# Matrix-LSTM key blocks overlapped with rows fetched by DMA, and the first attention's norm two heads later

## The reference

```python
# first block: the two attention outputs are normed and joined
mixed = jnp.concatenate([_rmsnorm(o_a, norm_fox_out[l]), _rmsnorm(o_b, norm_sb_out[l])], axis=-1)
# o_a: forgetting attention ("fox"); o_b: stick-breaking attention ("sb"), 8 heads

# second block: matrix LSTM, 4 heads of 96, once forward and once backward
dmat = jnp.where(tri, b[..., :, None] - b[..., None, :] + ib[..., None, :], -jnp.inf)
m_t = jnp.maximum(inter, dmat.max(axis=-1))
s = jnp.einsum("bhtd,bhsd->bhts", qb, kb) * jnp.exp(dmat - m_t[..., None])
...
h = num / jnp.maximum(jnp.abs(den), jnp.exp(-m_t))[..., None]
...
h = h_f + h_b
h = h * lax.rsqrt(jnp.mean(h * h, axis=-1, keepdims=True) + EPS)
h = h.reshape(B, N, M_WIDTH) * g_m * jax.nn.sigmoid(mo)
```

## Time and profile before

| | us |
|---|---|
| median of 3 runs | 1767.93 (1761.85 to 1769.10) |
| the profiled execution | 1768.98 |
| its span in the profile | 1767.2 |
| PE busy | 1677.7 (95%) |
| DVE busy | 1110.0 (63%) |
| ACT busy | 804.0 (45%) |
| POOL busy | 84.1 (5%) |
| mean granted PE clock | 0.969 |

### The profile page before, as it was taken

The page is one execution under the profiler, slowest core; times in us unless marked ns, Lnnn a source line. Parts: engine busy times, 40 slices in busy tenths (PEclk is TensorE's granted clock), DMA queues, the critical chain, the costliest instruction groups (busy, mean ns, idle before and its releaser), DMA issues.

```text
span 1767.2 us, 27194 instructions
## 1 busy us (share of the span) xinstructions
PE 1677.7 (95%) x9914; PEld 1398.0 (79%) x9914; DVE 1110.0 (63%) x1808; ACT 804.0 (45%) x1318; POOL 84.1 (5%) x140
## 2 busy tenths in 40 slices
PE   7999888999999999999899999999999998999997
PEld 7987477899999977766337788888887875589997
DVE  5544677768888888634665755555558835475564
ACT  5534444454444454344563542144225355566462
POOL 0000000000001000000200000000000001000000
PEclk9999899999999999999789999999999998799999
DMA  7634244357777732410003355455542420046562
GB/s 279 207 114 132 82 141 158 131 166 251 248 239 246 243 105 72 131 60 0 1 1 131 126 199 163 142 179 190 158 147 81 130 85 0 1 144 202 172 197 83
DMA packets 68921, 244.64 MB, mean 138 GB/s; under 512 B 7392, under 2 KB 10608, under 8 KB 68720
## 3 DMA queue, kind: packets, MB, share of 16 engines
q1 hardware_dynamic: 54000, 189.43, 32.2%
q0 software_dynamic: 14848, 54.21, 9.9%
HBM read 242.55 MB, written 1.06 MB: 138 GB/s over the span
## 4 chain that ended last, share of the span: by engine, by line
PE 80%; DVE 11%; ACT 5%; issue 3%; DMA 1%; DVEq 0%; SPq 0%; ACTq 0%
PE pair L948 79%; DVE uv L1596 1%; DVE wl L1556 1%; ACT wh L472 1%; DVE sq L1574 1%; DVE sq L1632 1%; PE pair L1116 1%; DVE small L1623 1%; DVE uh_f L1669 1%; ACT sq L500 1%; DVE ul L1585 1%; ACT sq L844 1%; ACT rstd L510 0%; ACT rstd L512 0%; ACT sq L542 0%
## 5 line engine op out<-in xcount | busy, mean ns | idle before, releaser
L948 PE MATMUL pair<-uh,wh 128*128 128x256 f32 (+3 forms) x1840 | 577.5, 314 | 16.1 <-DVE ul L1585 7.1
L1556 DVE TENSOR_TENSOR wl<-ring,wh 128x1024 fp32r<-128x1024 f32 x350 | 426.8, 1224 | 243.2 <-ACT wh L472 236.4
L948 PE MATMUL pair<-ul,wh 128*128 128x256 f32 (+3 forms) x1840 | 572.5, 311 | 0.0
L948 PE MATMUL pair<-uh,wl 128*128 128x256 f32 (+3 forms) x1840 | 572.2, 311 | 0.0
L472 ACT ACTIVATE wh<-ring 128x1024 fp32r<-128x1024 f32 x350 | 367.6, 1052 | 265.1 <-PE pair L948 261.4
L948 PEld LDWEIGHTS pair<-uh,wh 128*128 128x128 f32 (+1 forms) x1840 | 342.8, 186 | 50.8 <-issue 18.1
L948 PEld LDWEIGHTS pair<-uh,wl 128*128 128x128 f32 (+1 forms) x1840 | 342.9, 186 | 25.1
L948 PEld LDWEIGHTS pair<-ul,wh 128*128 128x128 f32 (+1 forms) x1840 | 342.7, 186 | 24.0
L948 PE MATMUL pair<-hh,wh 128*128 128x512 f32 (+1 forms) x512 | 172.6, 337 | 0.8
L948 PE MATMUL pair<-hl,wh 128*128 128x512 f32 (+1 forms) x512 | 172.0, 336 | 0.0
L948 PE MATMUL pair<-hh,wl 128*128 128x512 f32 (+1 forms) x512 | 172.0, 336 | 0.0
(11 more groups left out here) (254 smaller groups left out, 2197.8 us busy)
## 6 DMA issues: line engine op xcount, KB each, us to landing
ring<-in_w_stream SPq DMA_DIRECT2D x350, 512.0 KB, 3.9
uh_f<-in_mods POOLq DMA_DIRECT2D x48, 512.0 KB, 6.1
mod_w<-in_mods POOLq DMA_DIRECT2D x48, 512.0 KB, 3.8
table<-in_table SPq DMA_DIRECT2D x1, 1849.5 KB, 12.4
res<-in_x SPq DMA_DIRECT2D x4, 256.0 KB, 3.7
res<-in_mem SPq DMA_DIRECT2D x1, 1024.0 KB, 14.7
res<-in_ctx POOLq DMA_DIRECT2D x1, 1024.0 KB, 6.3
uv<-c_rows POOLq DMA_DIRECT2D x2, 512.0 KB, 6.6
```

The lines of the kernel that those rows point to most:

```text
L948: ins = pe.matmul(*operands, **flags)
L1556: tt(wl[:, s, :], ring[:, s, :], wh[:, s, :].bitcast(F32), ALU.subtract).then_inc(S("w_lo"), 1)
```

## The change

**Rows by transfer.** For each layer GpSimd writes the rows of both directions to a new DRAM tensor `ml_dram`. It reads each head's row of both directions back, repeated on 128 partitions, twice (`row_load`, 512 KB each): one copy for blocks 0 and 2, one for blocks 1 and 3, where masks are added in place. There are buffers for two heads; the loads of heads 2 and 3 wait until heads 0 and 1 have left theirs (`ml_e`), and they stand behind the 16 casts in GpSimd's queue. The row maximum comes likewise (`max_load`). `spread`, `head_m` and ACT's copies (L853) go.

**1/den by transfer.** For heads 0 to 2, GpSimd writes 1/den to `den_dram` and, once that has landed (`den_out`), reads it back over 96 partitions into `quot` (`quot_in`). Head 3 is still spread by PE (`last_spread`).

**Order.** PE makes the scores of block t + 1 ahead of the values of block t; DVE adds masks one block ahead. Both directions go in one instruction where they can. Head h's square, norm, root and value now run two heads later. The rounding of the other mixers' results moves into head 0's steps. In the output projection head 2's norm stands before k = 4 and `last_spread` before k = 6.

**Forgetting attention's norm.** PE's part moves from h == 2 to h == 4, ACT's root from 2 to 5, DVE's gain from 4 to 6; squares and their sum stay.

Of the loops over the four heads the diff shows the new lines only; the old loops stand in the listing above.

```diff
+        ML_STEPS = [(h, kb) for h in range(MH) for kb in range(4)]
...
-        rb, arg = [ml[:, d, :] for d in range(2)], [ml[:, 4 + d, :] for d in range(2)]
-        den, quot = [ml[MD:MD + 1, 2 + d, :] for d in range(2)], [ml[0:MD, 6 + d, :] for d in range(2)]
+        rb_even = [lw[:, 0:1024].rearrange("p (d t) -> p d t", d=2), ml[:, 0:2, :]]
+        rb = [rb_even, [ml[:, 2:4, :], ml[:, 4:6, :]]] * 2
+        mrow = mrow_at[MD:MD + 1]
+        den, quot = ml[MD:MD + 1, 6:8, :], ml[0:MD, 6:8, :]
...
+            def row_load(l, h, k):
+                if h >= 2:
+                    pool.wait_ge(S("ml_e"), 8 * (l * MH + h - 1))
+                pool.dma_start(rb[h][k], ml_dram[l, :, h, 0, :].rearrange("(o d) t -> o d t", o=1)
+                               .to_broadcast([P, 2, 512])).then_inc(S(f"rb_in{h}_{k}"), 16)
+            def max_load(l, h):
+                if h >= 2:
+                    pool.wait_ge(S("ml_min"), l * MH + h - 1)
+                k = 2 * (h % 2)
+                pool.dma_start(mrow[:, k:k + 2, :], ml_dram[l, :, h, 1, :].rearrange("(o d) t -> o d t", o=1)
+                               ).then_inc(S(f"max_in{h % 2}"), 16)
+            def den_spread(l, h):
+                out = den_dram[l, h, :, cols].rearrange("(o d) t -> o d t", o=1)
+                pool.wait_ge(S("ml_rden"), l * MH + h + 1)
+                pool.dma_start(out, den[:, :, cols]).then_inc(S("den_out"), 16)
+                pool.wait_ge(S("den_out"), 16 * (l * (MH - 1) + h + 1))
+                if h:
+                    pool.wait_ge(S("u_v"), value_count(f"y_{l}", MH + 2 + h - 1))
+                pool.dma_start(quot[:, :, cols], out.to_broadcast([MD, 2, cols.stop - cols.start])
+                               ).then_inc(S("quot_in"), 16)
             for l in range(NL):
                 cols = lin_cols(l)
+                for d in range(2):
+                    pool.wait_ge(S("ml_rows"), 2 * l + d + 1)
+                    pool.dma_start(ml_dram[l, d], rows[d][:, 3:5, :]).then_inc(S("rows_out"), 16)
+                pool.wait_ge(S("rows_out"), 32 * (l + 1))
+                pool.wait_ge(S("job_full"), JOBS.full(JOBS.number(f"va_{l}", 3)))
+                row_load(l, 0, 0)
+                for h in range(2):
+                    max_load(l, h)
+                pool.wait_ge(S("sm_s"), UNIT0["mlat1"] if l == 0 else len(UNITS))
+                pool.wait_ge(S("conv_done"), 8 * l + 8)
+                for h, k in ((0, 1), (1, 0), (1, 1)):
+                    row_load(l, h, k)
                 for j in range(2):
                     pool.wait_ge(S("u_l"), U_AT[f"y_{l}"] + MH + j + 1)
                     for q in range(4):
                         for dst, src in ((uh, yfh), (ul, yfl)):
                             pool.tensor_copy(dst[MD:P, 4 * j + q, cols],
                                              src[32 * q:32 * q + 32, j, cols]).then_inc(S("y_moved"), 1)
+                for h in range(MH - 1):
+                    if h + 2 < MH:
+                        for k in range(2):
+                            row_load(l, h + 2, k)
+                    den_spread(l, h)
+                    if h + 2 < MH:
+                        max_load(l, h + 2)
...
                 if h == 2:
                     for t in range(2):
                         square("fox", t, heads[:, 2 * t:2 * t + 2, :], P, 512)
+                if h == 5:
                     root("fox", P, T, 512)
...
+                def head_root(h):
+                    root(f"head_{l}_{h}", MD, n, MD)
...
+                act.wait_ge(S("sm_out"), units.stop)
+                for h, kb in ML_STEPS:
+                    exps(h, kb)
+                    if h == 0 and kb < 3:
+                        round_y(2 * kb)
+                        round_y(2 * kb + 1)
+                    if kb == 0 and h >= 2:
+                        head_square(h - 2)
+                    if kb == 1 and h >= 2:
+                        head_root(h - 2)
+                    if kb == 1 and h:
                         head_ln(h - 1)
+                    if kb == 2 and h:
+                        head_exp(h - 1)
+                    if kb == 2 and h >= 2:
                         head_round(h - 2)
                 head_ln(MH - 1)
+                head_square(MH - 2)
+                head_exp(MH - 1)
+                head_root(MH - 2)
                 head_round(MH - 2)
                 head_square(MH - 1)
+                head_root(MH - 1)
                 head_round(MH - 1)
...
-                if h == 2:
+                if h == 4:
                     pe.wait_ge(S("sm_out"), NF)
                     wait_emptied(pe, "xkv", 7)
...
+                def head_norm(h):
+                    norm(f"head_{l}_{h}", MD, n)
+                def last_spread():
+                    pe.wait_ge(S("ml_rden"), (l + 1) * MH)
+                    pe.wait_ge(S("norm_rstd"), NORM[f"head_{l}_{MH - 2}"] + 1)
                     for d in range(2):
+                        last = mm(bank[6 + d][0:MD, cols], ones[MD:MD + 1, 0:MD], den[:, d, cols], start=True, stop=True)
+                    last.then_inc(S("ml_bc"), 1)
+                for j in range(4):
+                    claim(f"mlstm_{l}", j)
+                keys(0, 0)
+                for t, (h, kb) in enumerate(ML_STEPS):
+                    if t + 1 < len(ML_STEPS):
+                        keys(*ML_STEPS[t + 1])
+                    if kb == 0 and h >= 2:
+                        pe.wait_ge(S("ml_sum"), l * MH + h - 1)
+                    values(h, kb)
+                    if kb == 0 and h >= 2:
+                        head_norm(h - 2)
                 s = p0 + N_IN2
...
-                for k in range(4):
+                for k in range(KT - 1):
+                    if k == 4:
+                        head_norm(MH - 2)
+                    if k == 6:
+                        last_spread()
                     for m in range(2):
                         output(early[m], m, k)
-                head_spread(MH - 1)
-                for k in range(4, KT - 1):
-                    for m in range(2):
-                        output(early[m], m, k)
-                norm(f"head_{l}_{MH - 1}", MD, n)
+                head_norm(MH - 1)
                 for m in range(2):
...
-                if h == 4:
+                if h == 6:
...
+                    a = rb[h][kb % 2]
+                    dve.wait_ge(S(f"rb_in{h}_{kb % 2}"), 16 * (l + 1))
                     for d in range(2):
-                        if kb == 0:
-                            dve.wait_ge(S("ml_b_in"), 2 * (l * MH + h) + d + 1)
-                        if kb:
-                            dve.wait_ge(S("ml_e"), 2 * (4 * (l * MH + h) + kb - 1) + d + 1)
-                        tc = CTX if kb < 2 else LAT
-                        tt(arg[d][:, tc], rb[d][:, tc], masks[d][:, kb % 2, :], ALU.add).then_inc(S("ml_arg"), 1)
+                        if kb >= 2:
+                            dve.wait_ge(S("ml_e"), 2 * (t - 2) + d + 1)
+                        tt(a[:, d, c], a[:, d, c], masks[d][:, kb % 2, :], ALU.add).then_inc(S("ml_arg"), 1)
...
+                    if h < MH - 1:
+                        dve.wait_ge(S("quot_in"), 16 * (l * (MH - 1) + h + 1))
+                    else:
+                        dve.wait_ge(S("ml_bc"), l + 1)
+                        ch.link(dve.tensor_copy(quot[:, :, cols],
+                                                pair[3][0:MD, :].rearrange("p (d t) -> p d t", d=2)[:, :, cols]))
+                    ch.link(tt(quot[:, :, cols], ml_pair(l, h)[0:MD, :, cols], quot[:, :, cols], ALU.mult))
...
+                args(0, 0)
+                for t, (h, kb) in enumerate(ML_STEPS):
+                    if t + 1 < len(ML_STEPS):
+                        args(*ML_STEPS[t + 1])
+                    if kb == 2 and h:
                         head_min(h - 1)
+                    weigh(h, kb)
+                    if h == 0 and kb < 3:
+                        rest_y(2 * kb)
+                        rest_y(2 * kb + 1)
+                    if kb == 1 and h >= 2:
+                        head_value(h - 2)
+                    if kb == 2 and h >= 2:
+                        head_rest(h - 2)
+                    if kb == 3 and h:
                         head_sum(h - 1)
                 head_min(MH - 1)
+                head_value(MH - 2)
```

171 lines of the change are left out of this document (45 added, 126 removed).

## The result

The changed kernel takes 1775.38 us (median of 8 runs, 1771.73 to 1781.70), the kernel before 1768.13 beside it (8 runs, 1761.85 to 1770.44). The ratio is 1.0052 with a 95% interval of 1.0033 to 1.0071: slower by half a per cent, where the prediction had 1767 and a slight gain. The range (1754 to 1781) holds the time; the direction is wrong.

What follows compares the result with a forecast made beforehand. PE, busy 95%, bounds the whole; in the three stretches touched, waits, the lower clock and a serial chain do. Terms -8.3 + 6.1 + 0.2 = -2.0 from the profiled 1768.98 give 1767.0 us; range 1754 to 1781.

Steps and rivals of the forecast that it cites:

- The stick-breaking stage, -8.3 us: Stick-breaking stage: the norm's move removes PE's 3.97 us wait; head 5's copy comes at 215.5 against 223.8.
- this takes the clock to stay at 1.00 once the wait is gone: Stick-breaking stage: the condition for -8.3 us; if the clock still drops, about -1.
- the first attention's norm brings little: Rival, stick-breaking stage: the clock still drops or the wait moves elsewhere, -1 instead of -8.3, 1774 us; chance 0.12.
- Layer 0, +6.1 us: Layer 0's matrix LSTM: late row load, two trips and longer tail outweigh the overlap; last row group 944.1 against 937.96.
- The loop: Layer 0's matrix LSTM: each head's serial loop takes 19.6 us with the trip, 21.5 at the low clock.
- The tail: End of layer 0's matrix LSTM: from head 3's first weighing at 900.7 to the last row group at 944.1.
- The round trip, 6.3 us: 1/den through DRAM in the matrix LSTM: 2.8 write plus 3.5 read; bounds 5.6 and 12.0; 5.9 in layer 1.
- Layer 1, +0.2 us: Layer 1's matrix LSTM: the same at half width; last row group at 1548.4 against 1548.20.
- The dearer trip: Rival, GpSimd's queue: six trips in the matrix LSTMs, each from 2.5 us more, +15, 1782 us; chance 0.18.
- The clock rival: Rival, matrix LSTMs: the clock stays up, the low-clock terms of 11.4 us go, 1755.6 us; chance 0.25.
- the overlap doesn't work: Rival, matrix LSTMs: exponentials still form the chain, only costs come, about 12 us more, 1779 us; chance 0.05.
- The rule of the Trainium skill: GpSimd's transfers: 2.0 us fixed plus bytes over 436 GB/s, 3.2 for 512 KB; a trip some 4.9, result near 1759.

Runs made afterwards that it cites:

- a_loads: The changed kernel with head 2's two row loads ahead of GpSimd's 16 casts, the first 1/den still behind them; 1764.68 us, 0.9984 of before.
- a_casts: The changed kernel with head 2's row loads first and GpSimd's casts behind the 1/den of heads 0 and 1, eight each; 1758.13 us, 0.9948 of before.
- e_pe2: a_casts with every head's 1/den spread by TensorE, no transfer of it, the spread ahead of the next head's first scores; 1743.62 us, 0.9878 of before.
- e_spin: a_casts with products nobody reads ahead of TensorE's waits in heads 2 and 3 of the matrix LSTM; 1757.70 us, 0.9952 of before.
- b_foxspin: The kernel before with only the norm's move, plus 8 unread products each at head 4 and step 8 of the stick-breaking stage; 1761.16 us, 0.9964 of before.
- a_nofox: The changed kernel with the forgetting attention's norm moves undone, leaving the matrix LSTM part alone; 1778.44 us, 1.0064 of before.

## Why the prediction was wrong, point by point

**What bounds the kernel.** Right: three stretches moved, by 2.2 to 8.9 us, and the rest by no more than its clock makes it differ between profiles.

**The stick-breaking stage, -8.3 us.** The step that failed is "this takes the clock to stay at 1.00 once the wait is gone". It was stated as a condition and then taken. The order has a further wait of 1.92 us at head 4, which doesn't show in the trace before, where the products around it ran slowed, and behind it the clock drops in all nine profiles that have the norm moved and no product added at that place. The size of 8.3 was nearly right for the condition: with the two waits filled, 7.2 us come (55.2 to 47.96). Without, some 2 us, closest to the rival "the first attention's norm brings little" (-1); that the profile after showed 5.7 was luck.

**Layer 0, +6.1 us; measured +8.9.** Head 2's first weighing ends at 881.3 (880.01 + 1.28), 39.0 us after the stage's start at 842.3, where the steps of the prediction give 34.3 from 844.9 to 879.2. The 4.7 us add up along the path: the casts start 9.2 us into the stage instead of 10.2 (-1.0), take 13.9 for 11.3 (+2.6; they lie beside VectorE's work of head 0), the write of 1/den behind the loads takes 7.3 for 3.7 (+3.6), and the rest -0.5. The row load, 6.0 for 3.8, lies beside the write. The write lands 0.17 us behind the second of the two loads in both layers, and without loads in flight it takes 1.9 us (a_loads), so the loads are what holds it. The mis-sized terms are the row load and the write behind it. The load was read off `mod_w`, 3.8, although `uv`, of the same kind (one DRAM row repeated over 128 partitions, and issued as a pair), stood beside it with 6.6. The change's loads took 5.6 and 7.4 in the median: 5.2 to 6.4 for the first of a group, and more for each one behind it. The reason given, that the queues were idle, was no reason: the only thing in the queue was the pair of loads itself, and it was as dear as `uv`.

The loop was right: 21.1 us from head 2's first weighing to head 3's (881.3 to 902.4), forecast 21.5, and the clock in it 0.66 and 0.68 as forecast. Its parts were less right than its sum: the trip took 5.5 us for 6.3. **The tail** was 41.8 us (902.4 to 944.2), forecast 43.4.

**The round trip, 6.3 us.** Too high for four trips of six, and below its lower bound of 5.6: 5.5 and 5.2 us in layer 0, 5.0 and 4.9 in layer 1. The 2.8 for "a transfer of nearly nothing" was drawn through one row of GpSimd's queue and one of SP's; the small write took 1.6 to land and 1.9 to the read's issue. The first trip in each layer takes 10.7 and 10.4 us, since the write stands behind 1 MB of row loads in the same queue. The prediction saw that the write stands behind both loads and gave it 0.9 us for that; it was 5.4.

**Layer 1, +0.2 us; measured +2.2.** The same term: from the end of the casts to the end of the write it was 8.7 us (1499.92 to 1508.59), forecast 5.0 (1495.1 to 1500.1); the shorter loop (14.0 and 13.1 us between sums for 15.2) gave a part back.

**The rivals.** The dearer trip was given 0.18 and named the right place, GpSimd's queue, but the wrong reason: not each trip, only those that are queued behind row loads and casts. Two trips of 10.7 and 10.4 are 8.5 us over the forecast of 6.3 each, where six of 8.1 would have been 10.8. The clock rival did not come true in the matrix LSTM: PEclk was 0.66 to 0.71 in layer 0's loop. That the overlap doesn't work is refuted by a_casts and e_pe2: with the same overlap and another queue order the same stages are faster than before, 91.3 and 61.8, then 83.7 and 52.2, for 92.7 and 66.1.

**The rule of the Trainium skill** on the SWDGE path ("DMA: Bandwidth & Descriptors", "Anatomy of one DMA — SWDGE (gpsimd) path") gives, as an estimate from its two figures, 3.2 us for 512 KB, 2.0 for 4 KB and 2.9 for 384 KB. The trace disagrees for repeated rows (5.6 and 7.4 in the median, 5.2 at the least) and fits roughly for the small write (1.6 for 4 KB) and the read of 384 KB (3.4). The rule on the shared port (the Trainium skill, "SBUF — State Buffer", "Who interferes with whom"), that the two engines lock each other out, fits in kind, but who lost changed. In the kernel before the adds lost, up to 0.84 us for 0.42. In the kernel after they took 0.41 to 0.42 beside the casts, and the casts grew from at most 1.01 us to 1.69. In a_loads the adds lost again, up to 0.83.

What stays open: what the low clock costs in the matrix LSTM, since e_spin kept it up there only in part, and the 2.5 us between the stick-breaking stage and layer 0's matrix LSTM. b_foxspin shows that stretch long too (619.4 for 615.2) without any row transfer, and it goes with the granted clock there (0.994 before, 0.986 after, 0.983 in b_foxspin), so that a cause in the change isn't shown.

**The sum.** From -2.0 to the measured +7.3 (1775.4 - 1768.1) it is 9.3 us: about 6 in the stick-breaking stage (some 2 us of gain on the mean for 8.3), 2.8 in layer 0 and 2.0 in layer 1, together 11, less what single profiles can't place.

## What to carry to other kernels

Before a transfer is put on a queue, write down everything that stands ahead of it there and price each by a row of its own kind (repeated row, same size), not by the queue's fastest row, and ask whether that row was of transfers issued one at a time; a short transfer on the critical path goes ahead of long loads and of engine work that has time. Where a wait is removed and the clock is to stay up, look for the next wait in the same engine's row: here one of 1.92 us was enough, and eight products that nobody reads (2.10 us), at exactly that place, brought what the move alone did not. And a spread by TensorE of 2 us plus a copy of 1.2 beat a DRAM trip of 5.5; in layer 0 it did so only once it stood ahead of other work in its queue.

## What the runs showed of the hardware that was not expected

- A load of one DRAM row repeated over 128 partitions (512 KB) landed 5.2 to 6.4 us after issue when it was the first of its group, and 6.8 to 8.8 as the second, with no weights in flight; the same bytes from 128 rows of their own, issued one at a time, took 3.8.
- A write of 4 KB took 1.9 us from issue to the next issue when alone and 7.3 us behind 1 MB of such loads in the same queue. In the kernel after it landed 0.17 us behind the last of them in both layers.
- PEclk fell behind a TensorE wait of 1.92 us, with the engine otherwise busy, in all nine profiles that had it, and stayed at 1.00 when eight products filled it. Behind a wait of 2.13 us it fell in six profiles of nine, and behind one of 1.08 us in a_nofox and not in the kernel before.
- GpSimd's casts of 32x512 took up to 1.69 us beside VectorE's work and 0.61 at the least. In that run VectorE's adds showed nothing of it; in the kernel before and in a_loads the adds took up to twice their 0.42 us instead.
- The first 175 us of the program, the same code in all kernels, ranged from 169.0 to 175.4 us between profiles, with the granted clock: single profiles of two kernels can't be subtracted across it.
